# Modulation rows as dot products on the vector engine: from the inversion into the projection

## What is computed

```
def ada_split(cond, w_mod, b_mod):
    m = jax.nn.silu(cond) @ w_mod + b_mod
    return jnp.split(m, 6, axis=-1)

sh1, sc1, gt1, sh2, sc2, gt2 = ada_split(c, w_mod, b_mod)      # 6 x 1024
csh1, csc1, _, _, _, _ = ada_split(c_ctx, w_mod, b_mod)
hx = rms_norm(x, g_pre_mix) * (1 + sc1) + sh1
hc = rms_norm(ctx, g_pre_mix) * (1 + csc1) + csh1
... prepare, scan and readout of the RWKV branch, pooling branch, merge ...
x = x + gt1 * rms_norm(mix, g_post_mix)
h2 = rms_norm(x, g_pre_ffn) * (1 + sc2) + sh2
x = x + gt2 * rms_norm(peer_ffn(h2), g_post_ffn)
```

## Time and profile before

| What | us |
|---|---|
| median of 3 runs | 2726.8 (2724.35 to 2730.57) |
| profiled execution, whole | 2722.86 |
| its span, first to last instruction | 2721.2 |
| `front`, 0 to 73.2 | 73.2 |
| `project`, 73.2 to 382.5 | 309.3 |
| `gates`, 382.5 to 533.1 | 150.6 |
| `invert`, 533.1 to 789.6 | 256.5 |
| `scan`, `mix`, `peer`, 789.6 to the end | 1931.6 |

### The profile page before, as it was taken

One profiled execution on the slowest core, in us unless ns is written; L12 is line 12 of the kernel. 1 busy time (PEld: TensorE's weight loads), 2 busy tenths in 40 slices (PEclk: granted clock), 3 DMA queues, 4 the chain that ended last, 5 costly groups with the idle time before them and its releaser, 6 DMA issues.

```text
span 2721.2 us, 41392 instructions
## 1 busy us (share of the span) xinstructions
PE 2194.2 (81%) x16681; PEld 1368.9 (50%) x16681; DVE 1633.0 (60%) x3421; ACT 855.9 (31%) x1668; POOL 713.1 (26%) x607
## 2 busy tenths in 40 slices
PE   6899959886758888879789888787887778777876
PEld 2777748665258777767545443333333333333332
DVE  2488964258202434345477578777777777777764
ACT  4476733244143332323322222212212212222211
POOL 0000037000011211200233344444344444444441
PEclk8899979975858999979889999888888899899899
DMA  4245453252435242234599999999999999999995
GB/s 171 88 162 215 180 213 113 105 204 91 141 128 201 88 149 89 80 117 147 206 392 386 372 347 421 411 420 421 421 420 420 420 421 420 421 420 421 421 421 217
DMA packets 128832, 741.53 MB, mean 273 GB/s; under 512 B 17120, under 2 KB 24320, under 8 KB 60032
## 3 DMA queue, kind: packets, MB, share of 16 engines
q0 software_dynamic: 73728, 536.90, 47.9%
q1 hardware_dynamic: 53760, 199.89, 20.2%
q10 hardware_dynamic: 1152, 2.10, 0.2%
HBM read 683.14 MB, written 55.69 MB: 272 GB/s over the span
## 4 chain that ended last, share of the span: by engine, by line
DMA 27%; PE 17%; DVE 3%; issue 2%; ACT 2%; POOL 1%; another core or an unknown queue 0%; DVEq 0%; ACTq 0%; POOLq 0%
DMA uvx<-in_uv_in,ic 24%; PE bank L2361 13%; DMA uv<-in_uv_in,ic 3%; DVE junk L2254 1%; PE bank L91 1%; PE bank L93 1%; PE bank L92 1%; PE bank L2340 1%; ACT dg L2169 0%; POOL uvx L2092 0%; ACT ge L2164 0%; ACT L2164 0%; DVE wql L2220 0%; DVE gc_ L2260 0%
## 5 line engine op out<-in xcount | busy, mean ns | idle before, releaser
L2361 PE MATMUL bank<-uv,dg 128*128 128x512 f32 x1664 | 811.2, 645 | 197.7 <-ACT dg L2169 193.9
L2361 PEld LDWEIGHTS bank<-uv,dg 128*128 128x128 f32 x1664 | 335.0, 206 | 664.0 <-issue 403.6
L2254 DVE SCALAR_TENSOR_TENSOR junk<-uv,gr 128x1024 f32<-128x1024 f32 x416 | 509.9, 1226 | 215.9 <-DMA uv<-in_uv_in,ic 192.2
L2092 POOL DMA_INDIRECT uv<-in_uv_in,ic x416 | 460.7, 1108 | 629.1 <-PE bank L2361 563.0
L2164 ACT ACTIVATE ge<-dt_ 128x4 f32<-128x4 f32 x128 | 26.3, 205 | 926.5 <-DVE junk L2254 926.4
L2361 PE MATMUL bank<-uvx,dg 128*128 128x512 f32 x384 | 208.3, 704 | 70.9 <-ACT dg L2169 70.9
L2361 PEld LDWEIGHTS bank<-uvx,dg 128*128 128x128 f32 x384 | 85.0, 228 | 194.2 <-issue 103.4
L2169 ACT ACTIVATE dg<-ident,gc_ 128x128 f32<-128x128 f32 x512 | 163.6, 390 | 29.5 <-DVE gc_ L2260 29.0
L91 PE MATMUL bank<-ht_hi,wh 128*128 128x256 f32 (+1 forms) x432 | 151.3, 350 | 22.9 <-DVE wl L553 22.9
L2092 POOL DMA_INDIRECT uvx<-in_uv_in,ic x96 | 109.2, 1137 | 167.0 <-PE bank L2361 158.1
L92 PE MATMUL bank<-ht_lo,wh 128*128 128x256 f32 (+1 forms) x432 | 146.3, 339 | 0.0
(11 more groups left out here) (334 smaller groups left out, 3858.6 us busy)
## 6 DMA issues: line engine op xcount, KB each, us to landing
pair_record<-rec SPq DMA_DIRECT2D x40, 768.0 KB, 3.3
wm<-in_wmod SPq DMA_DIRECT2D x16, 1024.0 KB, 5.2
wraw<-in_wpair_in SPq DMA_DIRECT2D x24, 512.0 KB, 3.6
ab<-pair_record SPq DMA_DIRECT2D x16, 768.0 KB, 6.2
wz<-in_wz_in SPq DMA_DIRECT2D x20, 512.0 KB, 3.4
wm<-in_wmod SPq DMA_DIRECT2D x4, 2048.0 KB, 21.6
wraw<-in_wq_in SPq DMA_DIRECT2D x16, 512.0 KB
uv<-in_uv_in,ic POOLq DMA_INDIRECT x416
```

The lines of the kernel that those rows point to most:

```text
L2092: pool.indirect_dma_start(ring(i), None, g["uv_in"], bass.IndirectOffsetOnAxis(ap=ic[:, s % ICR, k:k + 1], axis=0)).then_inc(su[row_slot[i ...
L2254: dve.scalar_tensor_tensor(junk[:, :], ring(i)[:, 0:D], 1.0, hc[:, t % 2, :], ALU.mult, ALU.mult, accum_out=dt[:, k:k + 1]).then_inc(s_ud, 1)
L2361: mm = pe.matmul(acc(t, c)[:, :], dg[:, n % 2, k, :], ring(i)[:, D + 512 * c:D + 512 * c + 512], start=h == 0 and q == 0 and k == 0, stop= ...
```

## The change

- The host lays the 16 MB out transposed: `wrow_in` is 32 tiles of 128 rows by 1024, and `c` comes in as a row of its own (`c_in`).
- `project` loads `c` to all 128 partitions; ACT makes the tanh of it (1024 wide) and DVE the product `silu`. A new DVE step `dot(m)` multiplies tile m with `silu`, scales by 0.5 and sums over the 1024 elements into column m of `mod_dots`. There are 32 of them, four in each pass of the DVE loop for j = 0 to 7.
- SP loads the tiles (512 KB each) into three buffers; `row_weights(m)` waits for `dot(m-3)`. Four of these stand in each pass of SP's loop.
- `columns` moves to DVE's tail of `project`, and with it the turn by PE, the copy by ACT and the store. The store is waited for ahead of the stage's end.
- `kf` has one buffer now in place of two; ACT's `rates(j)` therefore waits for `keys_out(j-1)`.
- In `invert`, `halves`, `row`, `column`, `columns`, the turn, the copy and the store are gone, with the waits on them.

The diff, cut to its core:

```
 def project(nc, sb, sem, g):
+    NM, MR = 4 * KT, 3
...
             def _(sp):
+                def row_weights(m):
+                    if m >= NM:
+                        return
+                    if m >= MR:
+                        sp.wait_ge(s_dot, m - MR + 1)
+                    sp.dma_start(wt[:, m % MR, :], g["wrow_in"][m]).then_inc(s_wt[m % MR], 16)
...
                 weights(2)
+                sp.dma_start(cond[:, :], g["c_in"].broadcast_to((P, D))).then_inc(s_cb, 16)
...
                 for n in range(3, 8):
                     weights(n)
+                for m in range(MR):
+                    row_weights(m)
                 for j in range(NPAIR + 1):
                     if j + 1 < NPAIR:
                         weights(3 * j + 8)
+                    row_weights(4 * j + 3)
                     if j:
                         sp.wait_ge(s_r, 2 * j)
                         stored("r", j - 1)
+                    row_weights(4 * j + 4)
...
+                    row_weights(4 * j + 5)
...
+                    row_weights(4 * j + 6)
...
+                sp.wait_ge(s_rw, 1)
+                sp.dma_start(rows_dram.rearrange("v (k p) -> (v k) p", p=P), rw[:, :]).then_inc(s_rst, 16)
+                sp.wait_ge(s_rst, 16)
...
             def _(act):
                         act.wait_ge(s_at, 4 * j + 2 * d + 2)
-                        act.activation(kf[:, j % 2, d, :], al[:, j % 2, d, :], ACT.Identity, bias=col(j, OKA),
+                        if j:
+                            act.wait_ge(s_k, 2 * j)
+                        act.activation(kf[:, d, :], al[:, j % 2, d, :], ACT.Identity, bias=col(j, OKA),
...
                 high(0)
                 high(1)
+                act.wait_ge(s_cb, 16)
+                act.activation(silu[:, :], cond[:, :], ACT.Tanh, scale=0.5).then_inc(s_cth, 1)
...
                 exps(NPAIR - 1)
+                act.wait_ge(s_ct, 1)
+                act.activation(rw[:, :], bank[6][0:NM, 0:P], ACT.Copy).then_inc(s_rw, 1)
...
             def _(dve):
+                def dot(m):
+                    if m >= NM:
+                        return
+                    dve.wait_ge(s_wt[m % MR], 16 * (m // MR) + 16)
+                    if m:
+                        dve.wait_ge(s_dot, m)
+                    dve.scalar_tensor_tensor(cond[:, :], wt[:, m % MR, :], 0.5, silu[:, :], ALU.mult, ALU.mult,
+                                             accum_out=mc[:, m:m + 1]).then_inc(s_dot, 1)
...
+                dve.wait_ge(s_cth, 1)
+                dve.scalar_tensor_tensor(silu[:, :], silu[:, :], 1.0, cond[:, :], ALU.add, ALU.mult).then_inc(s_si, 1)
+                dve.wait_ge(s_si, 1)
...
                         shift(3 * j + 3)
                         low(3 * j + 5)
+                    dot(4 * j)
                     if j:
                         unit(j - 1)
                         keys(j - 1)
                         queries(j - 1)
+                    dot(4 * j + 1)
                     if j < NPAIR:
                         summed(j)
                         shift(3 * j + 4)
                         low(3 * j + 6)
                         bounded(j)
+                    dot(4 * j + 2)
                     if j:
                         keys_out(j - 1)
                         bonus(j - 1)
                     if j < NPAIR:
                         shift(3 * j + 5)
                         low(3 * j + 7)
+                    dot(4 * j + 3)
+                    if j == NPAIR:
+                        columns()
                     if j:
                         removal(j - 1)
                         addition(j - 1)
...
             def _(pe):
                 bonus(NPAIR - 1)
+                pe.wait_ge(s_cv, 1)
+                pe.transpose(bank[6][0:NM, 0:P], colv[:, :, :].rearrange("p v k -> p (v k)"), ident[:, :]).then_inc(s_ct, 1)
...
 def invert(nc, sb, sem, g):
-                for n in range(EARLY + 1):
-                    halves(n)
                 stored(0)
-                for n in range(EARLY + 1, NR):
-                    halves(n)
...
-                        if b and u == HB - 10:
-                            columns()
...
-                    pe.wait_ge(s_rwc, NR if b else EARLY)
-                    if b:
-                        pe.wait_ge(s_rw, 1)
...
                 turned_in(1)
-                pe.wait_ge(s_ric, 32)
-                for n in range(EARLY):
-                    row(n)
                 turned_out(0)
                 combined(0)
-                pe.wait_ge(s_zc, 12)
-                column(0)
-                for n in range(EARLY, NR):
-                    row(n)
-                    column(n - 1)
-                column(NR - 1)
...
                 turned_out(1)
                 combined(1)
```

161 lines of the change are left out of this document (74 added, 87 removed).

## The result

The changed kernel takes 2709.4 us (median of 6 runs, 2696.8 to 2711.2); the kernel before, over the 6 runs measured with it, 2724.1 us (2719.1 to 2730.6). The ratio is 0.9933, 95% interval 0.9908 to 0.9958: faster by 0.7%, in the middle of the predicted range of 2700 to 2721 us. The profiled execution of the changed kernel took 2710.5 us with a span of 2708.8 us, against 2722.9 and 2721.2 before.

The account below looks back on a forecast made before the run. PE was taken to bound `project`, and DVE's break on PE's last late row to hold up `invert`. Inversion -43.5, projection +25.5 and clock +3 gave -15 us, forecast 2711.5 us from the median, range 2700 to 2721.

Parts of the forecast that it names:

- The inversion, -43.5: In `invert`, DVE's break for `columns` in its second inversion goes and `turned_out(1)` starts earlier: -43.5 us.
- DVE becomes the bound: In `project`, four dots raise DVE's work in a pair from 28.5 to 33.8 us, more than PE's 31.4.
- The other work of a pair, 28.5: In `project`, DVE's work in a steady pair without dots: 31.4 less 2.9 us of waits, 28.5 us.
- the hand-offs, 1.0: In `project`, DVE waits twice a pair for ACT's next tile, about 0.5 us each, 1.0 us a pair.
- pair 7 and the tail: End of `project`: four dots (5.3 us) and `columns` (1.5 us), with a wait of 2.96 shrinking to 0.5: +4.3 us.
- pair 0: First pair of `project`: its dots fit into DVE's waits of 2.58 and 6.04 us on ACT, at no cost.
- The clock, +3: In `project`, PE waits 2.6 to 3.1 us ahead of `lora(j, 1)`; half clock behind some waits costs 3 us.
- Loads, `kf`, tanh and silu at nothing: In `project`, the row-weight loads, the single `kf` buffer and the tanh and `silu` steps cost nothing.
- PE stays the bound: Rival in `project`: dots fit DVE's idle time, a pair grows by 2.0 us, 2699 us; chance 0.15 with nearby cases.
- The clock in every pair: Rival in `project`: PE's clock falls in every pair, +8 in place of +3, 2716.5 us; chance 0.20.
- half speed that lasts: Rival in `project`: clock stays at 0.50 through `product(3j+6)`, +64 us, 2747 us; chance 0.05 in full, 0.04 in part.
- the dot at half rate: Rival in `project`: a dot takes 2 x 1.23 us on DVE, +34 us, 2745 us; chance 0.02.

Follow-up runs that it names:

- the first two experiments: Changed kernel with the 32 dots left out and loads kept, 2688.5 us; changed kernel with dots kept and only the first three row-weight tiles loaded, 2707.5 us.
- the fourth: Changed kernel with all 32 dots, their loads, tanh, silu, `columns`, turn and store moved from the projection into gates: 2698.5 us, ratio 0.9906.
- a3: Changed kernel with two of the four dots of a pair moved to where DVE waits for ACT: 2692.8 us, ratio 0.9893 to the kernel before.

## Why the prediction was right

**The inversion, -43.5: right, -44.1.** The break on DVE and PE's late rows are gone, and `turned_out(1)` starts as soon as the inversion ends. The run with `columns` last shows that both had to go: with DVE's wait out of the inversion and PE's queue left as it was, only 10 us came back.

**DVE becomes the bound: right.** The dots' step was mis-sized. I took 1.33 us from the start-to-start of two dots in a row while saying that it may be 1.23 between other instructions; it is 1.145 (268.25 to 269.39). An instruction of another kind starts while the dot's end and its accumulator read are still shown. 24 dots in pairs 1 to 6 at 0.185 us less are 4.4 us of the miss.

**The other work of a pair, 28.5: 28.1, and the hand-offs, 1.0: 1.41.** Both are off by 0.4 us, for one reason: I read the brackets alone. A first shift behind a wait has its second 1.25 us behind it, before the change too (293.15 to 294.39 in the pair of the earlier trace rows), and 1.05 behind another instruction. Two such shifts a pair put 0.4 us into the 28.5 that belongs to the waits, and left it out of the hand-offs, so the sum of the two was right: 33.8 + 1.0 = 34.9 was forecast, 28.1 + 4.6 + 1.4 = 34.1 came, and the difference is the dots'. For the stage: 2.7 x 6 = 16.3 us where 20.9 stood, pair 7 and the tail +3.4 where 4.3 stood, pair 0 +0.6 where 0 stood, the row store 0.2 where 0.3 stood, the pair with the clock 1.2.

**The clock, +3: 1.2.** The waits ahead of `lora(j, 1)` came a little shorter than worked out, 2.2 to 2.7 us (2.6 to 3.1 forecast), and where the clock fell it cost 1.2 us, as in the run without loads 1.2 and 1.0 (1.0 to 1.3 forecast). The step that failed is the count, and with it the reasoning: I placed the wait between one of 1.47 us behind which the clock did not fall and one of 2.99 behind which it did, as if the length decided. Here it fell behind the wait of 2.23 us and not behind five of 2.30 to 2.67; in the run without loads in two pairs. In these rows the length of a wait does not tell whether the clock falls, and what does is left open.

**Loads, `kf`, tanh and silu at nothing: right**, shown by the first two experiments and the fourth.

**The rivals.** *PE stays the bound* was wrongly named: its pair of 33.4 us, for 2699 us, is longer than PE's 31.4 and is a DVE that works without a break. Such a DVE needs 32.7, so that rival lacked only the placing of two dots, and a3 at 2692.8 us is nearly its case. The clock in every pair, half speed that lasts, and the dot at half rate did not come; the last, which rested on the Trainium skill's page "Vector Engine (DVE) Microarchitecture Reference", section "Points that are easy to get wrong", would give 2.46 us as a factor on the row, and the 32 dots of the changed kernel take 1.21 to 1.23 us each. It was GpSimd that made dots slow, in a stage in which the change has none.

**What was to show it.** The inversion without a break, 212.4 us where about 213 stood, dots of 1.22, brackets of 0.45 and 0.54 where 0.4 to 0.6 stood: as said. The pair (34.14, where 34.9 to 36.2 stood) and project (330.9, where 335 to 343 stood) lie just below, for the dot's price and the clock. Of PE's waits in pairs 1 to 6 four (2.65 to 2.67 us) lie in the 2.6 to 3.1 and two (2.23 and 2.30) below.

**The total.** -15 was forecast and -12.4 came in the profiles, -14.7 and -18.6 in the medians. (From the median of 2726.8 the sum gives 2711.8, not the 2711.5 on record.) The projection was 7 us cheaper than thought and the late stages took back 5 to 13 us (by the medians 5 to 8, in the two profiles 10 and 13) that no step of mine had. That the sum came out within 1 to 4 us is in part luck.
